# A two-layer hybrid backbone on one core: the z projection between state-space steps, activation tables loaded at the norms, output groups ahead of the last mixer transposes, and head norms of the delta rule in three parts

## The chip, the cores and the metric

The kernel runs on one core of one Trainium2 chip. The metric is the device time of one execution in microseconds (us). The profile names the engines PE (TensorE, matmuls), PEld (its weight loads), DVE (VectorE), ACT (ScalarE), POOL (GpSimd) and SP (SyncE, which issues the weight transfers).

## What is computed

Two trunk layers over 256 context tokens and 256 latent tokens of width 1024, all in fp32. Layer 0 mixes tokens with Mamba-2 (SSD) heads and gated linear attention (GLA) heads side by side, layer 1 with the gated delta rule (GDN). Each layer has a modulated RMS norm ahead of the mixer and of the SwiGLU part, and one RMS norm ends the whole. Scans run forward and backward. The parts that matter here:

```python
def ssd_scan(xdt, da, bm, cm, s0):      # chunked Mamba-2
    ac = jnp.cumsum(da.reshape(b, nc, CHUNK, g, e), axis=2)
    decay = jnp.exp(jnp.where(tril[:, :, None, None], seg, -jnp.inf))
    scores = jnp.einsum('bclgn,bcsgn->bclsg', cc, bc)[..., None] * decay
    y_diag = jnp.einsum('bclsge,bcsgep->bclgep', scores, xc)
    states = jnp.einsum('bclgn,bclgep->bcgepn', bc, xc * to_end[..., None])
...
def even_mixer(...):
    z, xbc, dt_f, dt_b, q, k, v, r, gl_f, gl_b = split_cols(h @ w_in, EV_SPLITS)
...
    y = (y_ssd + d_skip[:, None] * xs).reshape(b, t, SSD_INNER) * jax.nn.silu(z)
    y = rms_norm(y.reshape(b, t, SSD_GROUPS, SSD_INNER // SSD_GROUPS), ...)
    o = rms_norm(y_gla, gla_nw).reshape(b, t, GLA_VAL) * jax.nn.silu(r)
    return jnp.concatenate([y, o], axis=-1) @ w_out
...
def reference(...):
    for i in range(DEPTH):              # 0: even mixer, 1: odd mixer (gated delta rule)
        hl = rms_norm(x, norm_mix[i]) * (1.0 + sc1) + sh1
        x = x + g1 * yl
        x = x + g2 * swiglu(rms_norm(x, norm_ffn[i]) * (1.0 + sc2) + sh2, ffn_w1[i], ffn_w3[i], ffn_w2[i])
    return rms_norm(x, final_norm)
```

## The kernel before

Each engine has its own hand-written program; semaphores join them. Activations are kept transposed, features on the partitions and the 512 tokens along the row, in 8 chunks of 128 features. Weights come in blocks of up to 1 MB through a ring of three slots (RING = 3): SP issues block n as soon as block n-3 is released (lines 647 to 664). A block is released when its two outputs are done ("done"), when it is the first half of something ("used"), or when modulation rows are done ("rows"). A group of a projection (gemm, line 719; gemm_tok, line 753) is one block: two PSUM outputs, f = 0 and f = 1, of 8 chunks each. An fp32 matmul shows as two records of PE. Outputs go round the PSUM banks 0 to 3; a bank is free again when ScalarE or VectorE has drained it.

The stages of layer 0 in TensorE's order: four modulation blocks with the first norm's sums, xbc (6 groups with convolution and transposes), small0, z0 (4 groups), the SSD loop (line 912), qk0 (4 groups), the transposes of the SSD output, v0 (4 groups, each behind a gates() product), r0 (4 groups, each behind the transposes of one key head), the GLA loop, its transposes, out0, the feed-forward stages ff0 and dn0. Layer 1: small1, qkv, z1, the GDN loop, transposes, out1, ff1, dn1. The remaining eight modulation pieces of layer 0 come as 16 late halves (line 690): each is a weight block of its own and 8 short records, put behind f = 0 of a group (between, line 711); LATE_AT gives the places. Before every second one, late_columns(q) turns a row into columns.

The SSD loop has 32 steps u: 8 tiles (4 per direction) of 2 groups of 2 half groups. A step is: POOL makes g_decay (line 2231), TensorE a decay product (line 923), ScalarE Exp (line 1411), VectorE the masked product p_seg (line 1908), TensorE four diagonal products (line 941). Every second step adds a pair: the product with the state (for k > 0) and the new state (lines 945 to 950). VectorE folds a pair into y0 and st0 (accumulate, line 1879). At every fourth step it makes the inputs xdt and xw (line 1872), of which there is one buffer each, after the accumulation of the step before. TensorE's order at a step is decay(u+1), wait for p_seg(u), diagonal products, pair.

Behind the loop VectorE multiplies y0 by z, ScalarE sums squares and makes the norm's scale (lines 1412 to 1417), VectorE scales y0 in 8 products (merged). Then VectorE takes the gates gk of v0 (line 1925), one for each gates() product of TensorE, which waits for the one before (line 966).

A norm (ScalarE, line 1326) waits for the residual of each chunk, squares it, TensorE sums (norm_sum), then ScalarE does Ln and Exp; VectorE scales and ScalarE shifts the chunks of hT one by one, and the first group behind the norm waits for each chunk in its f = 0 part (line 733). The tables of ScalarE are loaded by ACT_TABLE_LOAD, which the compiler puts ahead of an activation whose function is not in the loaded set.

In the GDN loop ScalarE squares the outputs of chunk 6 in steps 28 to 31 (line 1695), and after the loop makes the scales of its 16 heads, squares chunk 7, and makes the scales of those (lines 1697 to 1700). VectorE merges, TensorE transposes 16 tiles, and ScalarE copies each (mixed, line 1419). out0 and out1 have 16 chunks in two blocks per group; the first block reads tiles 0 to 7, which for out0 are SSD tiles.

## Time and profile before

| | us |
|---|---|
| median of 3 runs | 2292.64 (2291.91 to 2293.5) |
| the profiled execution | 2295.65 |
| its span in the trace | 2293.8 |
| PE busy | 2089.5 |
| DVE busy | 729.5 |
| ACT busy | 566.1 |

A row of the timeline has its start, its duration, the engine, the line, the operation, output<-input, the shape and type, the count of merged records, and in brackets how long the engine had been idle and what ended that. A row of the windows has the stretch, its length, the busy time of PE, PEld, DVE, ACT and POOL with the number of records, the granted TensorE clock as a share of full speed (0.50 is 1.2 GHz, 1.00 is 2.4 GHz), the busy share of the DMA engines and GB/s. Row times are us from the start of the span.

### The profile page before, as it was taken

The page shows a single profiled execution, that of the slowest core. Times are in us where ns is not written, and L with a number is a line of the kernel's source. Part 1 is how long each engine was busy: PE and PEld are TensorE (multiplying, and loading weights), DVE is VectorE, ACT ScalarE, POOL GpSimd, SP SyncE. Part 2 cuts the span into 40 slices and gives each one's busy share as a digit, 9 for nine tenths or more (in the row PEclk, how much of TensorE's full clock was granted, in tenths as well). Part 3 has the DMA queues.
Part 4 walks back from the last instruction along what each step waited for, and adds up shares of the span by engine and source line. Part 5 has one row for each costly group of instructions (what it writes and reads, how often), then busy time and mean ns, then how long its engine had stood idle before and what let it go on. Part 6 is the DMA issues. An engine that isn't in the chain of part 4 may idle for free.

```text
span 2293.8 us, 29492 instructions
## 1 busy us (share of the span) xinstructions
PE 2089.5 (91%) x12486; PEld 1289.4 (56%) x12486; DVE 729.5 (32%) x1474; ACT 566.1 (25%) x1217; POOL 79.6 (3%) x86
## 2 busy tenths in 40 slices
PE   6999766999999799999999998999898889799997
PEld 2468443488555544444444446544576556578886
DVE  2540665000444500100000004555686944210001
ACT  4121112141334400200000004222536766420001
POOL 0000220000000000000000000000102110000000
PEclk9999887999989899999999997999998999799999
DMA  6333000312343122122221122221120001134442
GB/s 250 147 115 147 1 0 2 148 55 108 122 158 148 38 74 83 55 73 73 78 87 69 64 70 77 92 74 55 56 75 3 2 2 56 55 119 157 147 146 93
DMA packets 28000, 193.53 MB, mean 84 GB/s; under 512 B 3004, under 2 KB 4285, under 8 KB 5854
## 3 DMA queue, kind: packets, MB, share of 16 engines
q1 hardware_dynamic: 27826, 191.51, 22.7%
q8 instruction: 99, 1.62, 0.3%
q14 instruction: 31, 0.25, 0.0%
q10 hardware_dynamic: 44, 0.14, 0.0%
HBM read 190.59 MB, written 1.05 MB: 84 GB/s over the span
## 4 chain that ended last, share of the span: by engine, by line
PE 81%; DVE 11%; ACT 5%; issue 2%; DMA 1%; POOL 0%; SPq 0%; ACTq 0%; DVEq 0%; POOLq 0%
PE psum L673 80%; DVE ws_sb L1746 4%; ACT ws_sb L1312 2%; DVE gl_tmp_sb L1746 1%; DVE arena_sb L1746 1%; DVE hT_sb L1749 1%; ACT L1312 1%; ACT arena_sb L1312 1%; ACT wide_sb L1312 1%; DVE ws_sb L1749 1%; DMA xT_sb<-x 1%; DVE ring_sb L1746 1%; ACT const_sb L1312 1%; ACT hT_sb L1312 0%; DVE arena_sb L1755 0%
## 5 line engine op out<-in xcount | busy, mean ns | idle before, releaser
L673 PE MATMUL psum<-hT_sb,ring_sb 128*128 128x512 f32 (+1 forms) x2256 | 810.6, 522 | 19.4 <-ACT hT_sb L1312 15.0
L673 PEld LDWEIGHTS psum<-hT_sb,ring_sb 128*128 128x128 f32 x2256 | 433.7, 193 | 389.3 <-issue 357.0
L673 PE MATMUL psum<-arena_sb,ring_sb 128*128 128x512 f32 (+1 forms) x1216 | 396.3, 488 | 3.6 <-DVE small_sb L1752 1.9
L1312 ACT ACTIVATE ws_sb<-psum 128x512 f32<-128x512 f32 (+3 forms) x268 | 148.6, 554 | 860.8 <-PE psum L673 853.1
L673 PEld LDWEIGHTS psum<-arena_sb,ring_sb 128*128 128x128 f32 x1216 | 232.7, 192 | 165.3 <-issue 144.1
L673 PE MATMUL psum<-ring_sb,hT_sb 128*128 128x256 f32 (+4 forms) x1312 | 251.8, 378 | 11.3 <-ACT hT_sb L1312 11.3
L673 PEld LDWEIGHTS psum<-ring_sb,hT_sb 128*128 128x128 f32 (+1 forms) x1312 | 207.8, 187 | 56.9 <-issue 20.0
L673 PE MATMUL psum<-ws_sb 128*32 128x32 f32 (+5 forms) x2352 | 143.4, 234 | 46.8 <-DVE ws_sb L1746 46.4
L673 PEld LDWEIGHTS psum<-ws_sb 128*32 128x32 f32 (+4 forms) x2352 | 117.3, 134 | 86.3 <-DVE ws_sb L1746 60.3
L1746 DVE TENSOR_TENSOR arena_sb<-ws_sb,psum 128x512 f32<-128x512 f32 (+1 forms) x44 | 24.4, 555 | 419.9 <-PE psum L673 419.9
L1749 DVE SCALAR_TENSOR_TENSOR xT_sb<-psum,mod_sb,xT_sb 128x256 f32<-128x256 f32 x48 | 23.2, 484 | 388.3 <-PE psum L673 387.7
L1312 ACT ACTIVATE wide_sb<-xT_sb 128x512 f32<-128x512 f32 (+1 forms) x40 | 21.8, 544 | 429.7 <-PE psum L673 296.2
L1749 DVE SCALAR_TENSOR_TENSOR ws_sb<-ws_sb,cols_sb 128x512 f32<-128x512 f32 (+1 forms) x176 | 123.8, 703 | 6.3
L673 PE MATMUL psum<-const_sb,arena_sb 64*128 64x256 f32 (+3 forms) x512 | 104.7, 418 | 6.2 <-ACT const_sb L1312 2.4
L673 PE MATMUL psum<-arena_sb,ws_sb 64*64 64x128 f32 (+1 forms) x640 | 97.6, 316 | 2.9 <-DVE ws_sb L1749 2.7
L673 PE MATMUL psum<-wide_sb,const_sb 128*32 128x256 f32 (+2 forms) x384 | 77.0, 476 | 20.4 <-DVE ws_sb L1755 5.8
L1312 ACT ACTIVATE arena_sb<-psum 128x512 f32<-128x512 f32 x56 | 33.4, 597 | 228.3 <-PE psum L673 221.4
L673 PEld LDWEIGHTS psum<-const_sb,arena_sb 64*128 64x128 f32 (+2 forms) x512 | 55.6, 188 | 49.2 <-issue 37.8
L673 PE MATMUL psum<-ws_sb,const_sb 128*64 128x256 f32 (+1 forms) x192 | 62.0, 540 | 18.7 <-ACT hT_sb L1312 15.4
L1312 ACT ACT_TABLE_LOAD x50 | 64.2, 1283 | 52.6 <-PE psum L673 33.3
L673 PEld LDWEIGHTS psum<-arena_sb,ws_sb 64*64 64x64 f32 (+1 forms) x640 | 64.4, 154 | 13.1 <-issue 7.2
L2216 POOL TENSOR_TENSOR wide_sb<-small_sb,const_sb 128x512 f32<-128x512 f32 x24 | 25.5, 1060 | 1331.8 <-PE psum L673 1317.6
(154 smaller groups left out, 1404.7 us busy)
## 6 DMA issues: line engine op xcount, KB each, us to landing
ring_sb<-w SPq DMA_DIRECT2D x170, 1024.0 KB, 4.8
ring_sb<-w SPq DMA_DIRECT2D x8, 768.0 KB, 4.0
xT_sb<-x SPq DMA_DIRECT2D x1, 2048.0 KB, 14.0
...
ring_sb<-w SPq DMA_DIRECT2D x2, 256.0 KB, 4.1
...
```

Of the source, the lines that this page charges most:

```text
L673: return nc.tensor.matmul(o, l, r, start=start, stop=stop)
L1312: return nc.scalar.activation(o, i, func, **kw)
L1746: return V.tensor_tensor(o, a, b, op)
L1749: return V.scalar_tensor_tensor(out=o, in0=a, scalar=sc, in1=b, op0=op0, op1=op1)
L2216: return G_.tensor_tensor(o, a, b, ALU.mult)
```

## The change

- z0 leaves its place ahead of the SSD loop. It is cut into 32 parts of 4 matmuls; parts 0 and 1 come ahead of the loop, part u+2 at step u between decay(u+1) and the wait for p_seg(u). ScalarE copies each of the 8 fills (z_copy) and applies Silu to all of z behind the loop. qk0 takes the place ahead of the loop.
- xdt and xw have two buffers; inputs(m+1) are made at step 4m+1. Each accumulation comes behind the next masked product. The state and the state product have one PSUM bank each instead of two, since z uses banks 2 and 3.
- The transposes of the SSD output and their copies move behind v0.
- The 16 late halves are placed anew: xbc 8 (two each in groups 4 and 5), qk0 4, r0 4.
- load_tables(5) at the start of every norm, behind z's Silu, behind the last GLA squares, and ahead of the last GDN squares.
- gemm_after: the first group behind mix0, ffn0 and ffn1 does both outputs for each chunk; small1 and the first query group are done together, chunk by chunk. Norms wait for drained banks in place of the "residual" count. The Sigmoid of beta comes behind Ln.
- out0's first block is multiplied ahead of the GLA transposes, out1's first block behind 10 of the 16 GDN transposes.
- The GDN squares begin at step 25; the scales of chunk 6 are made at step 29, those of 12 heads of chunk 7 behind the loop, the last four after that, and the merges of chunk 6 go into steps 30 and 31.

```diff
+LN_TABLES = 5
...
-LATE_AT = {"xbc": (0, 6), "z0": (6, 4), "qk0": (10, 4), "r0": (14, 2)}
+LATE_AT = {("xbc", 0): (0,), ("xbc", 1): (1,), ("xbc", 2): (2,), ("xbc", 3): (3,), ("xbc", 4): (4, 5), ("xbc", 5): (6, 7),
+           ("qk0", 0): (8,), ("qk0", 1): (9,), ("qk0", 2): (10,), ("qk0", 3): (11,),
+           ("r0", 0): (12,), ("r0", 1): (13,), ("r0", 2): (14,), ("r0", 3): (15,)}
...
+        if outs_end == "z":
+            self.n_z += 2
+            release = ("z", self.n_z)
...
-    with_late("z0", 4)
     with_late("qk0", 4)
+    p.stage("z0", [([(CB, KC)], "z")] * 4)
...
-        z0 = area(arena, 4096, TT, D)
+        z0 = area(arena, 0, TT, D)
...
-        xdt = area(ws, 5120, SSD_H, SSD_P)
-        xw = area(ws, 6144, SSD_H, SSD_P)
+        xdt = [area(w, at, SSD_H, SSD_P) for w, at in ((ws, 5120), (extra, 0))]
+        xw = [area(w, at, SSD_H, SSD_P) for w, at in ((ws, 6144), (extra, 1024))]
...
-        gate = ws[0:2 * RANK + 1, 1024:2048]
+        gate = extra[0:2 * RANK + 1, 2048:3072]
...
-                if n == plan.stages["z0"][0][0][0]:
+                if n == plan.stages["qk0"][0][0][0]:
                     sp.dma_start(const[:, 6:NCONST - 1, :], consts[:, 6:NCONST - 1, :]).then_inc(s_levels, 16)
...
-                if n % 2 == 0 and n > 0:
+                if n % 2 == 0 and n not in (0, 12):
                     late_columns(n // 2 - 1)
...
+                for half in LATE_AT.get((stage, g), ()):
+                    late_half(half)
+
+            def gemm_after(stage, src, lo, tag):
+
+                ids, first = plan.stages[stage][0]
+                w = slot(ids[0], CB, KC)
+                block_ready(ids[0])
+                for f in range(2):
+                    bank_free(first + f)
+                for c in range(KC):
+                    chunk_ready(tag, c)
+                    for f in range(2):
+                        last = mm(psum[:, (first + f) % 4, lo:T], w[:, c, f * P:(f + 1) * P], src(c),
+                                  start=(c == 0), stop=(c == KC - 1))
+                        if c == KC - 1:
+                            last.then_inc(s_done, 1)
+                between(stage, 0)
...
+                        if meanwhile:
+                            meanwhile()
...
+                    src = lambda c, s=span(stage, 2 * g): hT[:, c, s]
+                    if g > 0:
+                        gemm(stage, g, src, KC, lo=span(stage, 2 * g).start)
+                    elif stage == "xbc":
+                        gemm_after(stage, src, 0, "mix0")
...
-            def small1():
+            def small1_and_first_queries():
+
                 ids, b = plan.stages["small1"][0]
                 w = slot(ids[0], 64, KC)
                 block_ready(ids[0])
                 bank_free(b)
-                for j in range(TT):
-                    for c in range(KC):
-                        if j == 0:
-                            chunk_ready("mix1", c)
-                        last = paired_mm(psum[:, b % 4, j * 64:(j + 1) * 64], c, j, w[:, c, :])
-                last.then_inc(s_done, 1)
+                q_ids, first = plan.stages["qkv"][0]
+                wq = slot(q_ids[0], CB, KC)
+                block_ready(q_ids[0])
+                for f in range(2):
+                    bank_free(first + f)
+                s = span("qkv", 0)
+                for c in range(KC):
+                    chunk_ready("mix1", c)
+                    for j in range(TT):
+                        last = paired_mm(psum[:, 4 + j, 0:64], c, j, w[:, c, :])
+                    if c == KC - 1:
+                        last.then_inc(s_done, 1)
+                    for f in range(2):
+                        last = mm(psum[:, (first + f) % 4, s], wq[:, c, f * P:(f + 1) * P], hT[:, c, s],
+                                  start=(c == 0), stop=(c == KC - 1))
+                        if c == KC - 1:
+                            last.then_inc(s_done, 1)
...
+            def z0_part(n):
+
+                fill, sub = n // 4, n % 4
+                g, f, bank = fill // 2, fill % 2, 2 + fill % 2
+                block = plan.stages["z0"][g][0][0]
+                w = slot(block, CB, KC)
+                if sub == 0:
+                    if f == 0:
+                        block_ready(block)
+                    if fill >= 2:
+                        pe.wait_ge(S["z_taken"], fill - 1)
+                j = 2 * f + sub // 2
+                for c in range(sub % 2 * 4, sub % 2 * 4 + 4):
+                    last = mm(psum[:, bank, sub // 2 * CB:(sub // 2 + 1) * CB], hT[:, c, j * P:(j + 1) * P], w[:, c, :],
+                              start=(c == 0), stop=(c == KC - 1))
+                if sub == 3:
+                    last.then_inc(S["z_done"], 1)
...
-                pe.wait_ge(S["late_copied"], 5)
-                pe.wait_ge(S["late_taken"], 4)
+                late_columns(5)
                 edges(0)
+                pe.wait_ge(S["late_taken"], 6)
...
                 last.then_inc(S["ssd_bc"], 1)
+                for g in (2, 3):
+                    for i in range(2):
+                        drained(pe, out_of("qk0", g, i))
+                z0_part(0)
+                z0_part(1)
                 pe.wait_ge(S["ssd_masked"], 4)
                 pe.wait_ge(S["edge"], 1)
...
+                    if u + 2 < 32:
+                        z0_part(u + 2)
...
+                        if v > 0:
+                            pe.wait_ge(S["ssd_y"], v)
                         if k > 0:
-                            mm(psum[:, 2 + v % 2, :], cT[:, g, j * P:(j + 1) * P], st0[:, g])
-                        last = mm(psum[:, v % 2, :], b_tok[:, j, g * P:(g + 1) * P],
-                                  xw[:, g * 8:(g + 1) * 8].rearrange("p a b -> p (a b)"))
+                            mm(psum[:, 1, :], cT[:, g, j * P:(j + 1) * P], st0[:, g])
+                        last = mm(psum[:, 0, :], b_tok[:, j, g * P:(g + 1) * P],
+                                  xw[m % 2][:, g * 8:(g + 1) * 8].rearrange("p a b -> p (a b)"))
...
-                for j in range(2 * D_FF // CB):
-                    gemm(f"ff{i}", j, lambda c: hT[:, c, lo:T], KC, lo=lo, after=f"ffn{i}" if j == 0 else None)
+                gemm_after(f"ff{i}", lambda c: hT[:, c, lo:T], lo, f"ffn{i}")
+                for j in range(1, 2 * D_FF // CB):
+                    gemm(f"ff{i}", j, lambda c: hT[:, c, lo:T], KC, lo=lo)
...
             for g in range(4):
-                gemm_tok("z0", g, (0, 1, 2, 3))
+                gemm("qk0", g, lambda c: hT[:, c, :], KC)
             ssd()
...
-            pe.wait_ge(S["late_taken"], 6)
+            pe.wait_ge(S["ssd_exp"], 32)
+            pe.wait_ge(S["z_taken"], 8)
             for g in range(4):
                 gates(g)
+                if g == 1:
+                    pe.wait_ge(S["ssd_y"], 16)
                 gemm_tok("v0", g, (0, 1, 2, 3))
+            transpose_mix("ssd", y0, 8, TT)
             pe.wait_ge(S["gk"], TT)
+            pe.wait_ge(S["mixed"], 8)
             for g in range(4):
                 key_tokens(g)
                 gemm_tok("r0", g, (0, 1, 2, 3))
+            late_columns(LATE - 1)
             gla()
-            transpose_mix("gla", o0, 8, TT)
-            pe.wait_ge(S["mixed"], 16)
-            gemm_and_norm("out0", lambda c: mixT[:, c, :], 16, "ffn0")
...
+
+            def gla_transposes():
+                transpose_mix("gla", o0, 8, TT)
+                pe.wait_ge(S["mixed"], 16)
+
+            pe.wait_ge(S["gla_taken"], 16)
+            gemm_and_norm("out0", lambda c: mixT[:, c, :], 16, "ffn0", gla_transposes)
             ffn(0)
-            small1()
+            small1_and_first_queries()
...
-            transpose_mix("gdn", o1, 16, 2)
-            pe.wait_ge(S["mixed"], 32)
-            gemm_and_norm("out1", lambda c: mixT1[:, c, :], 16, "ffn1")
+
+            def gdn_transposes():
+                transpose_mix("gdn", o1, 16, 2, 10)
+                pe.wait_ge(S["mixed"], 32)
+
+            transpose_mix("gdn", o1, 10, 2)
+            pe.wait_ge(S["mixed"], 24)
+            gemm_and_norm("out1", lambda c: mixT1[:, c, :], 16, "ffn1", gdn_transposes)
...
+            def load_tables(n):
+
+                nc.scalar.add_instruction(mybir.InstLoadActFuncSet(name=nc.get_next_instruction_name(), ins=[], outs=[], act_func_set_id=n))
...
+                load_tables(LN_TABLES)
...
-                        act.wait_ge(S["residual"], (n - 1) * KC + c + 1)
+                        drained(act, out_of(NORM_OF[tag], c // 2, c % 2))
...
+            def z_copy(fill):
+
+                act.wait_ge(S["z_done"], fill + 1)
+                g, f_ = fill // 2, fill % 2
+                own(f(z0[:, 2 * f_:2 * f_ + 2, g * CB:(g + 1) * CB], psum[:, 2 + fill % 2, :].rearrange("p (a b) -> p a b", a=2),
+                      ACT.Copy).then_inc(S["z_taken"], 1), S["z_taken"])
...
+                    if u % 4 == 3:
+                        z_copy(u // 4)
+                for i in range(2):
+                    z = z0[:, 2 * i:2 * i + 2]
+                    ins = f(z, z, ACT.Silu)
+                own(ins.then_inc(S["z_ready"], 1), S["z_ready"])
+                load_tables(LN_TABLES)
...
-            def gla():
...
+                    if stage == "r0":
+                        mixed("ssd", 8, 0, lambda t: cl("ssd_norm", t), mixT, T)
...
+                load_tables(LN_TABLES)
...
-                link(f(beta, beta, ACT.Sigmoid))
                 log1p_exp_neg_abs(te, das, S["ab_ln"])
+                own(f(beta, beta, ACT.Sigmoid).then_inc(S["beta"], 1), S["beta"])
...
+                    if i >= 25:
+                        squares(6 + (i - 25) // 4, (i - 25) % 4)
+                    if i == 29:
+                        head_scales(16, 32)
+                head_scales(0, 12)
+                load_tables(LN_TABLES)
+                squares(7, 3)
+                head_scales(12, 16)
...
+            act.dma_start(gate, gate_in).then_inc(s_gate, 16)
+            keys_and_queries()
...
+                def inputs(m):
+
+                    d, k = m // 4, m % 4
                     j = TILE_AT[d][k]
                     xj = x0[:, j].rearrange("p (h c) -> p h c", c=SSD_P)
-                    link(tt(xdt, xj, bc(dt[:, j, d * 16:d * 16 + 16], 2, SSD_P), ALU.mult))
-                    own(tt(xw, xdt, bc(edge[:, j, d * 16:d * 16 + 16], 2, SSD_P), ALU.mult).then_inc(S["ssd_x"], 1), S["ssd_x"])
+                    link(tt(xdt[m % 2], xj, bc(dt[:, j, d * 16:d * 16 + 16], 2, SSD_P), ALU.mult))
+                    own(tt(xw[m % 2], xdt[m % 2], bc(edge[:, j, d * 16:d * 16 + 16], 2, SSD_P), ALU.mult).then_inc(S["ssd_x"], 1), S["ssd_x"])
...
+                inputs(0)
                 for u in range(32):
                     d, k, g, hq = u // 16, u // 4 % 4, u // 2 % 2, u % 2
-                    if u % 4 == 0:
-                        if u > 0:
-                            accumulate(u // 2 - 1)
-                        inputs(d, k)
                     dve.wait_ge(S["ssd_exp"], u + 1)
                     if u - 1 > 0:
                         dve.wait_ge(S["ssd_diag"], u - 1)
                     own(tt(p_seg[:, u % 2], e_seg[:, u % 2], bc(g_mask[:, d, g, TILE_AT[d][k]], 1, 4), ALU.mult).then_inc(S["ssd_p"], 1), S["ssd_p"])
-                    if u % 4 == 3:
+                    if u % 2 == 0 and u > 0:
                         accumulate(u // 2 - 1)
+                    if u % 4 == 1 and u < 28:
+                        inputs(u // 4 + 1)
                 accumulate(15)
+                dve.wait_ge(S["z_ready"], 1)
...
+                def merge(i, heads):
+
+                    dve.wait_ge(S["mix_rs"], 3 if i == 1 else 4 if heads[0] < 12 else 5)
+                    for h in heads:
+                        o = o1[:, i, h * P:(h + 1) * P]
+                        ins = stt(o, o, stat[:, i * 16 + h:i * 16 + h + 1], z1[:, i, h * P:(h + 1) * P], ALU.mult, ALU.mult)
+                        if i == 0:
+                            own(ins.then_inc(S["merged"], 1), S["merged"])
...
+                    if i >= 30:
+                        merge(1, range(8 * (i - 30), 8 * (i - 29)))
+                merge(0, range(12))
+                merge(0, range(12, 16))
...
+            dve.wait_ge(S["beta"], 1)
```

## Rows read from the trace of the kernel before

**Rows 1.** Page, parts 1 and 4: busy time and chain.

```profile
PE 2089.5 (91%) x12486; PEld 1289.4 (56%) x12486; DVE 729.5 (32%) x1474; ACT 566.1 (25%) x1217; POOL 79.6 (3%) x86
...
PE 81%; DVE 11%; ACT 5%; issue 2%; DMA 1%; POOL 0%; SPq 0%; ACTq 0%; DVEq 0%; POOLq 0%
```

**Rows 2.** Windows by stage: stretch, its us, busy us by engine, PEclk, DMA.

```profile
158.10:219.50 61.40, 61.40 (x304) 50.91 (x304) 8.18 (x20) 10.94 (x17) 2.08 (x2) 1.00 0.31 120
...
227.60:386.40 158.80, 104.80 (x377) 64.31 (x376) 99.86 (x120) 19.11 (x32) 32.19 (x30) 0.81 0.00 1
386.40:450.30 63.90, 63.87 (x176) 27.59 (x177) 10.30 (x11) 14.23 (x29) 0.00 (x0) 0.96 0.26 101
...
457.50:523.40 65.90, 65.84 (x277) 53.02 (x278) 4.90 (x4) 26.01 (x28) 0.00 (x0) 0.97 0.14 48
...
781.90:798.80 16.90, 6.34 (x33) 4.79 (x33) 9.73 (x22) 9.60 (x16) 0.00 (x0) 0.70 0.01 1
...
1953.00:1978.70 25.70, 9.29 (x32) 4.68 (x33) 10.61 (x33) 20.73 (x60) 0.00 (x0) 0.54 0.00 0
```

**Rows 3.** Timeline, TensorE: late modulation half, z group, one SSD period.

```profile
181.01 1.04 PE L673 MATMUL psum<-ring_sb,small_sb 128*2 128x512 f32 x8
181.98 14.08 PE L673 MATMUL psum<-ring_sb,hT_sb 128*128 128x256 f32 x64
...
271.42 1.97 PE L673 MATMUL psum<-ws_sb 128*128 128x64 f32 x8 [7.20 <-DVE ws_sb L1746]
...
276.14 1.94 PE L673 MATMUL psum<-ws_sb,arena_sb 128*128 128x512 f32 x4
```

**Rows 4.** Timeline, VectorE, the same SSD period.

```profile
268.16 1.22 DVE L1746 TENSOR_TENSOR ws_sb<-arena_sb,small_sb 128x1024 f32<-128x1024 f32 x1
...
275.98 0.96 DVE L1746 TENSOR_TENSOR ws_sb<-ws_sb 128x512 f32<-128x512 f32 x1 [3.88 <-ACT ws_sb L1312]
...
280.70 0.69 DVE L1746 TENSOR_TENSOR ws_sb<-psum,small_sb 128x512 f32<-128x512 f32 x1
...
288.40 1.23 DVE L1746 TENSOR_TENSOR ws_sb<-arena_sb,small_sb 128x1024 f32<-128x1024 f32 x1
```

**Rows 5.** Timeline behind the SSD loop: VectorE and ScalarE.

```profile
386.41 4.42 DVE L1746 TENSOR_TENSOR arena_sb<-arena_sb 128x4096 f32<-128x4096 f32 x1
...
396.95 1.28 ACT L1312 ACT_TABLE_LOAD   x1
...
400.17 5.78 DVE L1746 TENSOR_TENSOR arena_sb<-arena_sb,small_sb 128x512 f32<-128x512 f32 x8 [9.33 <-ACT small_sb L1312]
...
464.21 1.23 DVE L1749 SCALAR_TENSOR_TENSOR arena_sb<-psum,ws_sb 128x1024 f32<-128x1024 f32 x1 [36.41 <-ACT ws_sb L1312]
```

**Rows 6.** Two large transfers at 107.7 to landing; page part 6, small ones.

```profile
DMA to landing us min/median/max: 4.7/5.8/6.9
...
ring_sb<-w SPq DMA_DIRECT2D x2, 256.0 KB, 4.1
```

**Rows 7.** Table load behind ffn0's sum (timeline); windows of the first feed-forward group.

```profile
916.08 1.28 ACT L1312 ACT_TABLE_LOAD   x1 [1.26 <-PE psum L673]
...
921.80:927.50 5.70, 5.62 (x7) 2.50 (x8) 5.31 (x12) 5.37 (x11) 0.00 (x0) 0.50 0.00 0
927.50:938.70 11.20, 11.20 (x27) 4.95 (x26) 0.86 (x2) 3.58 (x6) 0.00 (x0) 1.00 0.00 0
```

**Rows 8.** Windows: small1, then the first queries of layer 1.

```profile
1401.20:1410.50 9.30, 9.30 (x68) 8.95 (x69) 0.00 (x0) 0.00 (x0) 0.00 (x0) 0.50 0.00 0
1410.50:1428.30 17.80, 17.80 (x78) 15.31 (x77) 10.49 (x31) 8.93 (x16) 0.00 (x0) 0.85 0.34 122
```

**Rows 9.** Timeline at the two mixer ends.

```profile
788.22 8.30 DVE L1749 SCALAR_TENSOR_TENSOR hT_sb<-hT_sb,small_sb,arena_sb 128x256 f32<-128x256 f32 x16 [4.15 <-ACT small_sb L1312]
...
1953.59 1.28 ACT L1312 ACT_TABLE_LOAD   x1
...
1966.84 6.16 DVE L1749 SCALAR_TENSOR_TENSOR hT_sb<-hT_sb,small_sb,arena_sb 128x128 f32<-128x128 f32 x16 [5.73 <-ACT small_sb L1312]
```

123 lines of the change are left out of this document (42 added, 81 removed).

## The prediction

> **What bounds the kernel now.** I read the page's busy shares and its chain first. TensorE is busy 91% of the span and carries 81% of the chain; VectorE carries 11%, ScalarE 5% [rows 1]. So two things can pay: stretches in which TensorE stands idle or runs slowly, and work that can be moved into them. The stages come next [rows 2]. The state-space (SSD) loop, 227.6 to 386.4, is the one large hole: 158.8 us, of which TensorE is busy 104.8, at a granted clock of 0.81. The z projection just before it (158.1 to 219.5) and the key and query projection behind it (386.4 to 450.3) are solid matmuls. The other holes are the two mixer ends, 16.9 us with 6.3 busy and 25.7 with 9.3 busy.
>
> **Inside the SSD loop.** Between two tiles TensorE waits 7.20 us for VectorE [rows 3]. VectorE then runs in a row the two accumulations of a tile, the two input products and the next masked product: the input product starts at 268.16 and again at 288.40, a period of 20.24 us for four steps [rows 4]. The work of VectorE in a period is 4 masked products of 0.96, 2 accumulations of 5 operations (0.69 to 0.99, together 3.75 with their gaps) and 2 products of 1.23: 13.9 us. TensorE's is, at full clock, 4 decays of 0.86 (two records of 0.43; the pair of four takes 1.77 from start to start), 4 diagonal groups of 0.86 to 1.0 and 2 pairs of 1.77: 10.5. The loop is bound by neither, but by their taking turns.
>
> **1. z into the loop, queries before it.** The whole z projection is 128 matmuls; 32 of them (64 records) take 14.08 us, one part of four 1.72 [rows 3], 32 parts 55. New loop on TensorE at full clock: 55 + 32 decays 27.5 + 32 diagonals 27.5 + 16 pairs 24.8 (four have half the work) = 134.8. Is it then bound by TensorE? Let a pair end at 0. TensorE does decay, part and diagonal until 3.4, decay and part until 6.0, then needs the masked product. VectorE starts its accumulation at 0.1, ends at 3.85, and has the product at 4.85: 1.2 us to spare. The next pair needs that accumulation (one bank instead of two), there since 3.85. With the double xdt and xw the inputs (2.5) follow, the next product is ready at 8.35, and the pair ends at 8.65. So yes. Added: 2.5 for the first parts at the half clock at which the stage before ends, 2.1 at the end, where steps 30 and 31 have no part to fill them. 139.4 from the end of the B-C products (227.6) to the last pair. ScalarE's eight z copies (0.6) and two Silu have room: it is busy 19.1 of 158.8 [rows 2].
> What hid the rest before was the query stage, and it is gone from there. Behind the last pair VectorE accumulates (3.8), multiplies by z (4.42); ScalarE sums squares (6.0, until the load at 396.95), then Ln, an Exp load and Exp 1.8 (its Ln load now lies ahead: 1.28 less); VectorE merges 5.8 [rows 5] and only then, in order, takes the first gate tile, 1.23: done at 23.4. ScalarE's gate work (4.5) ends at 20.7, inside that. TensorE has two gate matmuls, 1.9, and the first value group, 14.0: at 15.9 it reaches the second gates, which wait for that tile. A new stall of 7.5, and 2.3 of half clock after it. Value stage: 4 x 15.9 + 9.8 = 73.4, against 65.8 [rows 2]; the 8 SSD transposes cost 7.1 as before.
> Sum from 227.6 to the start of r0: before 523.4 - 227.6 = 295.8, after 139.4 + 73.4 + 7.1 = 219.9: **-75.9**. The query stage ahead of the loop takes the z stage's place with the same 128 half-length matmul times and four late halves: 0.
>
> **2. The late halves of the modulation.** Sixteen as before; two more with a column step go to xbc, a column step to the SSD head, two halves to r0: +5.6 (0.97 a half [rows 3], 0.87 a column step), which the -75.9 had counted as removed. But xbc groups 4 and 5 now carry two halves each, and the ring has three slots. The block of group 5 is then the third behind that of group 4 and can only be asked for when group 4 is done; before, one other block lay between. The transfer lands 4.7 us after its issue [rows 6], 0.2 is issue, 0.87 of transposes hide it: 4.0 us of wait. The same for the small block behind group 5: the page's two such transfers have a median of 4.1 [rows 6], one of them behind a large one (5.7), so 2.5 alone: 1.8 of wait. Half clock after them: 2.7. **+8.5** (+4 to +12). On SP's queue the level masks (2 MB) are now issued behind the small block; the next weight block behind them has the small projection's 17 us. The last column step ends r0: +0.5.
>
> **3. Tables early at the norms.** Each norm has a load of 1.28 for Ln between the sum of squares and Ln (916.08), and another for Exp [rows 7]. The first now runs while ScalarE waits for the squares: five norms x 1.28 = **-6.4**. In the gated-attention scales the load still follows the last squares in ScalarE's order: 0. The removed "residual" step was not last in its wait: 0.
> The record of a load is 1.28 and the Ln starts at once after it. The Trainium skill, ScalarE: Activation LUTs, "What ACT_TABLE_LOAD costs", adds a drain of 1.38 to every switch; by it the five would give 13.3 and the sum would be some 7 us lower. The rows show no such gap.
>
> **4. Both halves of the first group per chunk.** The old first half was paced by the norm's chunks, 1.07 us each, so 8.7 instead of 7.0. But TensorE comes out of the norm's idle time at the half clock: 5.7 us at 0.50 behind ffn0 [rows 7]. Old: one group until 938.7, 16.9 us. New: 16 x 0.87 + half of 5.7 = 16.8. The wait for chunks had hidden the half clock; now it shows. **0** at mix0, ffn0 and ffn1 (-1.5 to +0.5 each).
>
> **5. small1 with the first queries.** The small projection runs 9.3 us at clock 0.50 with TensorE full, and the first query groups still have part of the half clock (0.85 over 17.8 us) [rows 8]. New, a chunk is 12 small records (0.10 hot, 0.14 cold) and 4 of 0.215: 1.9 hot, 3.4 cold. From 1391.3, a chunk and a half cold and the others hot: first group done at 1409.4, 10.7 before the old 1420.1. The second group, the edge sums, then the third group at 1417.7, which needs the first bank drained: ScalarE's chain behind small1 sheds two loads (no switch to the sigmoid and back), and that is at 1416.6. Old 1428.3: **-10.6**, 1.3 of it the Ln load counted in 3: **-9.3** here. Of this -2 to -10 is open, since what clock the mix gets no row shows.
>
> **6. Output groups ahead of the transposes.** At out0 TensorE idles from 781.9, while ScalarE and VectorE make the norm and merge (788.22, 8.30 us) [rows 9]. The first half of group 0 reads only SSD tiles: 16 x 0.87 = 13.9, from 783.6 to 797.5; then the 8 transposes 7.2, to 804.7, where the old kernel has that half done at 812.7: **-8.0**.
> At out1 ScalarE's chain is the limit: after the loop (1953.59) a pair of loads with the first norm, 16 squares, a second pair, and merges from 1966.84 [rows 9]. New: the first two parts go into the loop, where ScalarE has 1.6 to 2.1 us free per step and squares need 1.75; the scales at step 29 (3.1) do not fit and push the end by 2. Then scales of 12 heads until 1958.6, a load, 4 squares, the last scales until 1963.5, and only then the copies of the transposes, which are behind them in ScalarE's order. Ten tiles until 1970.2, first half 7.0 + 1.8, six tiles 4.1: 1983.3 against 1987.5: **-4.2** (-6 to 0).
>
> **Sum.** The terms: -75.9 + 5.6 + 8.5 + 0.5 - 6.4 - 9.3 - 8.0 - 4.2 = -89.2. The profiled execution took 2295.65 us (span 2293.8, the rest lies around it): 2206.4. The median of the runs is 3.0 below that execution: 2203.4, say 2203.5.
>
> **Rivals.** (a) The loop keeps its turns: some wait I did not see takes the place of the removed one, and four steps still take 20.2 (for: one bank now serves every pair; against: 1.2 us spare): loop 162, +22: 2226. Chance 0.10. (b) **Slower than before**: the parts do not lift the clock. At half clock a part is 3.4, a decay 1.7, a diagonal 1.8, a pair 3.5: 17.3 a pair, 277 for the loop: 2341. It decides from a loop of 229 us on, 7.1 a step. Against: the z stage of the same matmuls ran at 1.00 [rows 2]. 0.03. (c) The early load does nothing, because the Ln load is placed again: +6.4 and 1.3 behind the loop: 2211. 0.07. (d) The mix of 5 stays at the half clock: 8 x 3.4 = 27 instead of 18: 2212. 0.10. (e) One load serves Ln and Exp, and the Exp loads go too, about eight on the path, 9 us: 2194. That is the rule of the Trainium skill, ScalarE: Activation LUTs, "Table sets: the hidden batching unit": a set exists that holds both. The trace has two loads wherever Exp follows Ln [rows 7], and the diff names one set only. 0.05. The forecast as worked out has 0.65.
>
> **Chances.** Faster by over 0.2% (about what a measurement here can tell from no change) 0.96, same 0.01, slower 0.03. Range: ring waits, clock and mixer ends move the sum by -10 to +12, and (a), (c), (d), (e) lie at 2194 to 2226: 2190 to 2226.
>
> **What would show it.** TensorE near full at clock 1.0 in the loop, about 139 us to the last pair; a wait of 7 to 8 us before the second gates; waits for ring_sb of 4 and 2 us around xbc group 5; one table load, not two, behind each norm's sum; no gain in the first group of ffn0. It is wrong if the loop's TensorE still waits for masked products, or if the clock stays at 0.5 in loop or mix.

## The result: 2228.8 us, 63.5 faster, where 89 were forecast

| | before | changed | ratio, 95% |
|---|---|---|---|
| median | 2292.27 (4 runs) | 2228.82 (4 runs, 2223.81 to 2232.25) | 0.9722 (0.970 to 0.9745) |
| the same kernels, measured again | 2293.21 | 2226.86 (4 runs, 2219.6 to 2229.96) | 0.9697 (0.9672 to 0.9722) |
| profiled execution, its span | 2295.65, 2293.8 | 2232.25, 2230.4 | |

The forecast was 2203.5, with a range of 2190 to 2226; the time lies 2.8 us above its upper end. Below, experiments are compared with the changed kernel by their ratios to the kernel before; its own is taken as 0.971, the middle of the two, and 0.001 is 2.3 us. With intervals of about 0.002 each, a difference of 6 us or less between two of them is not told apart by times, and is read from the traces.

Page of the changed kernel, parts 1 and 4, as [rows 1] of before:

```profile
PE 2088.2 (94%) x12486; PEld 1288.1 (58%) x12486; DVE 724.1 (32%) x1442; ACT 571.8 (26%) x1221; POOL 88.1 (4%) x86
...
PE 85%; DVE 7%; ACT 5%; issue 1%; DMA 1%; POOL 0%; SPq 0%; ACTq 0%; DVEq 0%; POOLq 0%
```

TensorE's busy time is what it was (2089.5), in a span 63 us shorter: idle time went, and VectorE's share of the chain fell (11% to 7%). The DMA engines have 1% of the chain in both pages; in the changed kernel a part of it is the weight ring (`DMA ring_sb<-w 1%` by line), which the page of before does not list among its lines of 1%.

Where the time went, by the start of the same instruction in each trace. The changed kernel has two traces:

| stretch | forecast | first trace | second trace |
|---|---|---|---|
| start to xbc | -1.3 | -1.6 | -1.1 |
| xbc, to the small projection | +8.6 | +12.2 | +11.8 |
| small projection to the B-C products (their half clock was booked with the ring) | +3.6 | +6.5 | +5.7 |
| B-C products to GLA | -73.5 | -70.8 | -71.8 |
| GLA loop | 0 | +6.2 | +1.7 |
| out0 up to Exp of ffn0 | -9.3 | -9.6 | -9.6 |
| to Exp of mix1 | -1.3 | -1.2 | -1.1 |
| small1 and qkv | -9.3 | +4.3 | +4.3 |
| GDN, out1, to Exp of ffn1 | -5.5 | -6.8 | -6.7 |
| to the end | -1.3 | -2.7 | -2.7 |
| sum | -89.3 | -63.5 | -69.5 |

One edit that was to give 9.3 costs 4.3: 13.6 of the 26 us missed. The rest is in the stages ahead of the loop (6.5), in GLA (6.2 or 1.7) and between the B-C products and GLA (2.7 or 1.7), against some 3 us gained beyond the forecast at the other norms and mixer ends.

**The state-space loop** did what was forecast. Windows of the changed kernel (columns as in [rows 2]) and its timeline of one pair:

```profile
244.90:385.20 140.30, 137.53 (x634) 100.60 (x633) 96.94 (x115) 30.20 (x44) 40.58 (x30) 0.99 0.09 31
```

```profile
254.15 1.89 PE L680 MATMUL psum<-ring_sb,hT_sb 128*128 128x256 f32 x8
255.88 1.00 PE L680 MATMUL psum<-ws_sb 128*128 128x64 f32 x8
256.72 1.08 PE L680 MATMUL psum<-ws_sb,arena_sb 128*128 128x512 f32 x2
257.63 1.02 PE L680 MATMUL psum<-ws_sb,const_sb 128*128 128x512 f32 x2
258.49 1.89 PE L680 MATMUL psum<-ring_sb,hT_sb 128*128 128x256 f32 x8
260.21 1.00 PE L680 MATMUL psum<-ws_sb 128*128 128x64 f32 x8
```

Part (1.73 from start to start), diagonal, new state, decay, part: no idle time in brackets, where [rows 3] has 7.20. 140.3 us at clock 0.99 against 139.4 forecast.

**The waits of TensorE** between xbc and GLA, longest first (what was waited for, us in total, times, longest), and the value stage:

```profile
PE psum L680 <- DVE arena_sb L1838: 6.8, 1, 6.8
PE psum L680 <- DMA ring_sb<-w: 6.2, 2, 4.0
PE psum L680 <- ACT hT_sb L1384: 3.0, 1, 3.0
PE psum L680 <- DVE ws_sb L1835: 2.8, 1, 2.8
```

```profile
401.29 5.77 DVE L1835 TENSOR_TENSOR arena_sb<-arena_sb,small_sb 128x512 f32<-128x512 f32 x8 [7.99 <-ACT small_sb L1384]
407.09 1.22 DVE L1838 SCALAR_TENSOR_TENSOR arena_sb<-psum,ws_sb 128x1024 f32<-128x1024 f32 x1
408.37 3.78 PE L680 MATMUL psum<-extra_sb,gl_tmp_sb 33*128 33x512 f32 x4 [6.80 <-DVE arena_sb L1838]
412.08 16.41 PE L680 MATMUL psum<-ring_sb,hT_sb 128*128 128x256 f32 x64
```

The 6.8 is the predicted wait before the second gates (7.5): VectorE merges 5.77, then takes the gate tile, then TensorE goes on. Behind it a value group takes 16.41 instead of 14.08 and the gate product 3.78 instead of 1.98: 4.1 of half clock, where I had 2.3. The ring's waits were forecast as 4.0 and 1.8 and are 4.04 and 2.14.

**The mix** of small1 and the first queries, timeline and window:

```profile
1334.45 1.74 PE L680 MATMUL psum<-ring_sb,hT_sb 128*64 128x64 f32 x12 [4.78 <-ACT hT_sb L1384]
1335.98 2.02 PE L680 MATMUL psum<-hT_sb,ring_sb 128*128 128x256 f32 x4
1337.93 2.14 PE L680 MATMUL psum<-ring_sb,hT_sb 128*64 128x64 f32 x12
```

```profile
1334.40:1365.40 31.00, 30.95 (x130) 22.00 (x131) 9.14 (x22) 7.25 (x15) 0.00 (x0) 0.51 0.03 6
```

TensorE is busy 30.95 of 31.0 us, and yet its clock stays at the lower of its two levels: 3.88 a chunk, eight times. All nine traces of kernels with this mix behind this norm have it at the low clock, with lengths within 0.7 us of each other. This was rival (d), at 4 us worse than its price of 27.

### The profile page after: what moved, and what is told of

It reads as the page before. It is cut to its first block, busy times and chain, and to the rows that moved or that the text cites. A ratio compares the mean times of both kernels' runs of the same rounds, so it can differ in the third digit from the quotient of the medians.

```text
span 2230.4 us, 29470 instructions
## 1 busy us (share of the span) xinstructions
PE 2088.2 (94%) x12486; PEld 1288.1 (58%) x12486; DVE 724.1 (32%) x1442; ACT 571.8 (26%) x1221; POOL 88.1 (4%) x86
## 4 chain that ended last, share of the span: by engine, by line
PE 85%; DVE 7%; ACT 5%; issue 1%; DMA 1%; POOL 0%; SPq 0%; ACTq 0%; DVEq 0%; POOLq 0%
PE psum L680 85%; ACT ws_sb L1384 2%; DVE ws_sb L1835 1%; DVE gl_tmp_sb L1835 1%; DVE arena_sb L1835 1%; ACT arena_sb L1384 1%; DMA ring_sb<-w 1%; DMA xT_sb<-x 1%; DVE ws_sb L1838 1%; ACT L1384 1%; ACT wide_sb L1384 1%; ACT const_sb L1384 1%; DVE ring_sb L1835 0%; ACT hT_sb L1384 0%; DVE arena_sb L1844 0%
## 5 line engine op out<-in xcount | busy, mean ns | idle before, releaser
L680 PE MATMUL psum<-ring_sb,hT_sb 128*128 128x256 f32 (+4 forms) x1312 | 263.4, 382 | 6.9 <-ACT hT_sb L1384 4.8
L680 PEld LDWEIGHTS psum<-ring_sb,hT_sb 128*128 128x128 f32 (+1 forms) x1312 | 212.3, 189 | 70.5 <-issue 34.5
L680 PE MATMUL psum<-ws_sb 128*32 128x32 f32 (+5 forms) x2224 | 115.2, 225 | 0.2 <-issue 0.2
L680 PE MATMUL psum<-arena_sb,ws_sb 64*64 64x128 f32 (+1 forms) x640 | 104.0, 329 | 3.0 <-DVE ws_sb L1838 2.7
L680 PEld LDWEIGHTS psum<-ws_sb 128*32 128x32 f32 (+4 forms) x2224 | 90.2, 124 | 14.8 <-issue 9.0
L680 PEld LDWEIGHTS psum<-arena_sb,ws_sb 64*64 64x64 f32 (+1 forms) x640 | 68.2, 160 | 15.4 <-issue 7.5
L680 PE MATMUL psum<-ws_sb,const_sb 128*64 128x256 f32 (+1 forms) x192 | 51.6, 474 | 15.5 <-ACT hT_sb L1384 15.5
## 6 DMA issues: line engine op xcount, KB each, us to landing
xT_sb<-x SPq DMA_DIRECT2D x1, 2048.0 KB, 13.9
```

What stands on the lines that cost most here:

```text
L680: return nc.tensor.matmul(o, l, r, start=start, stop=stop)
```

## The experiments

In short: the forecast's terms for the state-space loop, the waits of the ring, the gates and the mixer ends hold; the mix fails by its cold start alone; and the waits that the change leaves are removable, down to 2177 us.

### Which parts give what: e1, e2, e3, e12

e1_z_alone keeps the z parts and the late halves and takes everything else back. e2_small1_alone takes back the mix, e3 the explicit loads, e12 the ends of both mixers (for GDN the old squares from step 28 and two `head_scales`, too). e1 is these three together with the old first groups:

```diff
-            small1_and_first_queries()
+            small1()
...
             def load_tables(n):
-                nc.scalar.add_instruction(...)
+                pass
...
-            pe.wait_ge(S["gla_taken"], 16)
-            gemm_and_norm("out0", lambda c: mixT[:, c, :], 16, "ffn0", gla_transposes)
+            gla_transposes()
+            gemm_and_norm("out0", lambda c: mixT[:, c, :], 16, "ffn0")
...
-            transpose_mix("gdn", o1, 10, 2)
-            pe.wait_ge(S["mixed"], 24)
+            transpose_mix("gdn", o1, 16, 2)
+            pe.wait_ge(S["mixed"], 32)
```

> Parts 1 and 2 alone: the z projection in the state-space loop and the new places of the late halves; everything else (early tables, both halves of a first group per chunk, small1 with the first queries, output groups ahead of transposes, head norms in three parts) is as in the kernel before. By the terms of the forecast: 2292.3 - 75.9 + 5.6 + 8.5 + 0.5 = 2231. By the trace of the changed kernel: between the starts of xbc and r0 it is 54.0 us shorter, r0 is 1.9 longer, and the GLA loop behind it, the same instructions, 6.2 longer. If those 6.2 belong to the change: 2292.3 - 54.0 + 1.9 + 6.2 = 2246; if they are only where the clock happened to fall in that execution: 2240.

Measured 2238.57, ratio 0.9757 (0.9735 to 0.9779), 56 us faster than before; the trace's GLA loop took 194.3. So the z move gives some 56 of the 61 forecast for it, and the 6.2 of GLA do not follow from z alone.

> The changed kernel with the small projection of layer 1 by itself again and the first query group behind it. By the forecast's step 5 this is 9.3 us slower than the changed kernel: 2238. By the trace of the changed kernel, where the mix ran at a clock of 0.50 from its first record to its last and a chunk took 3.88 us, the edit of step 5 cost 3.4 us instead of giving 9.3: this kernel should be 3.4 us faster, 2225.

Measured 2221.04, ratio 0.9671 (0.9648 to 0.9694): 9 us faster than the changed kernel, not slower. From the Exp of mix1 to the first GDN mask it takes 255.9 us; the changed kernel 260.4, the kernel before 256.1. 4.5 of the 9 are the mix; the others lie in stages that the edit does not touch.

> The changed kernel without its explicit table loads; where ScalarE needs a table it is loaded at the use. By the forecast's step 3: five norms at 1.28 and one load behind the state-space loop, 6.4 to 7.7 slower, 2235 to 2236.5. By a drain of 1.38 added to every switch, as the Trainium skill (ScalarE: Activation LUTs, What ACT_TABLE_LOAD costs) has it, 13 to 16 slower, 2242 to 2245. If the scales of GDN gain from their explicit load too, 1.3 more.

Measured 2233.92, ratio 0.9728 (0.9705 to 0.975), 4 us slower. In the traces each norm is 1.3 slower: TensorE waits 4.21, 5.88 and 4.91 us for the first chunk behind mix0, ffn0 and ffn1, against 2.96, 4.60 and 3.64. The last stretch is 2.3 longer, of which 1.1 is the clock in the feed-forward products behind ffn1 (154.7 against 153.6). Nothing like 13 to 16: the drain of 1.38 that the Trainium skill has (ScalarE: Activation LUTs, "What ACT_TABLE_LOAD costs") is not seen here.

> The changed kernel with both mixer ends as before: all transposes ahead of out0 and out1, and the head norms of the delta rule in two parts. By the forecast's step 6: 8.0 + 4.2 = 12.2 slower than the changed kernel, 2241. By the traces: out0 up to the norm behind it 8.3 to 9.6, out1 and the loop ahead of it 4.4 to 5.1: 13 to 15 slower, 2242 to 2244. If the three parts of the head norms cost in the loop what they give behind it, 8: 2237.

Measured 2234.57, ratio 0.9735 (0.9709 to 0.9761), 6 us slower, no more than the scatter. By the traces: from the GLA loop to the Exp of ffn0 137.3 against 129.3, 8.0, as forecast. From the first GDN mask to the Exp of ffn1 it took 391.1; eleven traces with the new end and table set 5 took 385.1 to 390.3, 387.6 on average: 3.5, where 4.2 was forecast. That difference is smaller than the scatter of the stretch, and the trace of the changed kernel (390.2) happens to be at its upper end.

### What filling the loop gives: e10

```diff
-                z0_part(0)
-                z0_part(1)
+                for n in range(32):
+                    z0_part(n)
...
-                    if u + 2 < 32:
-                        z0_part(u + 2)
```

> The changed kernel with all 32 z parts ahead of the state-space loop (55 us) and none in it; the double buffers, the one bank for the pair and the order of VectorE stay as changed. It tells what of the gain is the filling and what the new order. By the forecast's working the new order alone removes the turns: VectorE's 13.9 per four steps then bound the loop, 8 x 13.9 = 111, with z 166, against 140 in the changed kernel: 26 slower, 2255. If the turns stay without the filling (20.2 per four steps, 162, with z 217) it is 77 slower: 2306. Since TensorE idles in the loop, its clock falls in either case; at a clock near 0.8 TensorE's 10.5 become 13, still under VectorE's.

Measured 2259.28, ratio 0.985 (0.9826 to 0.9875): 32 us slower than the changed kernel. Windows of z and of the loop:

```profile
240.00:294.00 54.00, 54.00 (x252) 47.54 (x251) 4.69 (x6) 4.18 (x7) 0.00 (x0) 1.00 0.17 59
294.00:418.00 124.00, 95.76 (x379) 54.86 (x377) 91.25 (x109) 25.65 (x37) 36.13 (x30) 0.91 0.03 9
```

The loop takes 15.5 a period of four steps: neither the 20.2 of the turns nor VectorE's 13.9. The new order and the double buffers gave 4.7 a period, 38 us; filling gave the rest, 178 - 140 = 38, of which 32 are left in the time of the whole. What holds a period at 15.5 is not shown here.

### The ring: e4

One late half in each xbc group, half 6 behind the last group, half 7 between the two parts of the small projection:

```diff
-LATE_AT = {("xbc", 0): (0,), ("xbc", 1): (1,), ("xbc", 2): (2,), ("xbc", 3): (3,), ("xbc", 4): (4, 5), ("xbc", 5): (6, 7),
+LATE_AT = {("xbc", 0): (0,), ("xbc", 1): (1,), ("xbc", 2): (2,), ("xbc", 3): (3,), ("xbc", 4): (4,), ("xbc", 5): (5,),
...
+                        if (stage, g) == ("xbc", 5):
+                            late_half(6)
...
                 last.then_inc(s_done, 1)
+                late_half(7)
                 bank_free(b + 1)
```

> The changed kernel with one late half in each xbc group, one behind the last xbc group and one between the two parts of the small projection, so that no two of these blocks stand between two large ones. The trace of the changed kernel has waits of 4.04 and 2.14 us for the ring and 1.8 us of half clock behind the first. If the ring of three is their cause they go, but for about 1 us ahead of the small projection: 7 us faster, 2222. If the transfers were limited by the memory rather than by the release of a slot, the same bytes are due in the same time and the waits only move: 2229. If the half clock in the small projection comes from the wait ahead of it, about 3 us more go: 2219; if it comes from its own narrow matmuls, it stays.

Measured 2217.99, ratio 0.9662 (0.964 to 0.9683), 11 us faster than the changed kernel. Its timeline and windows:

```profile
140.02 1.04 PE L684 MATMUL psum<-ring_sb,small_sb 128*2 128x512 f32 x8
140.99 1.09 PE L889 MATMUL psum<-const_sb,arena_sb 128*128 128x128 f32 x8
142.09 10.98 PE L684 MATMUL psum<-ring_sb,hT_sb 128*128 128x32 f32 x64
```

```profile
142.00:144.00 2.00, 1.99 (x18) 1.91 (x18) 1.89 (x4) 0.00 (x0) 0.00 (x0) 1.00 1.00 414
146.00:154.00 8.00, 8.00 (x42) 7.21 (x42) 1.48 (x5) 0.63 (x1) 0.00 (x0) 0.50 0.71 297
```

No wait for the ring is left; the small projection starts 9.3 us sooner (142.09 against 151.37), 1.0 of it because half 7 now comes behind its first part. The release of the slots was the cause, not the memory. But the clock still falls some 3 us into the narrow matmuls, with no idle time ahead, and stays low for some 9 us, against 12.7 in the changed kernel: most of this loss was not the ring's, and my half clock of 2.7 stood under the wrong cause.

### The value stage: e5

```diff
                 own(tt(y0, y0, z0, ALU.mult).then_inc(S["summed"], 1), S["summed"])
+                gate_rows(0)
                 dve.wait_ge(S["mix_rs"], 1)
```

and, on ScalarE, the first `log1p_exp_neg_abs` ahead of the wait for `summed` (the squares then write elsewhere, and the explicit table load at that place goes).

> The changed kernel, but ScalarE does the first gate tile before it waits for the product y0 times z, and VectorE takes that tile between this product and the merges. In the changed kernel TensorE waits 6.8 us for that tile and then runs at half clock, which costs 1.8 in the gate matmuls and 2.3 in the second value group. If the in-order queues of ScalarE and VectorE are the cause, as the forecast had it, all of it goes: 10.9 faster, 2218. If the clock would have fallen there anyway, 6.8 faster, 2222. If the merges, now later, hold up the transposes behind the value stage, less; they are due some 50 us later, so I expect none of that.

Measured 2214.71, ratio 0.964 (0.9627 to 0.9654), 16 us faster. From the first to the last gate product 47.8 against 59.3 us: 11.5, the wait and its half clock, as expected; the other 4 to 5 are elsewhere and within the scatter. VectorE now takes the tile early:

```profile
384.79 4.42 DVE L1835 TENSOR_TENSOR arena_sb<-arena_sb 128x4096 f32<-128x4096 f32 x1
389.25 1.22 DVE L1838 SCALAR_TENSOR_TENSOR arena_sb<-psum,ws_sb 128x1024 f32<-128x1024 f32 x1
396.91 1.98 PE L680 MATMUL psum<-extra_sb,gl_tmp_sb 33*128 33x512 f32 x4
397.27 5.78 DVE L1835 TENSOR_TENSOR arena_sb<-arena_sb,small_sb 128x512 f32<-128x512 f32 x8 [6.80 <-ACT small_sb L1384]
```

### One table for Ln and Exp: e7

```diff
-LN_TABLES = 5
+LN_TABLES = 6
```

> The changed kernel with table set 6 in place of set 5 in its explicit loads. The Trainium skill (ScalarE: Activation LUTs, Table sets: the hidden batching unit) says that one set holds both Ln and Exp. By my rival (e) the Exp loads behind the explicit ones go: five norms, the SSD scales, the GLA scales and the last GDN scales, 8 loads of 1.28, of which 7 to 8 are on the path: 9 to 10 faster, 2219. By the other reading the compiler puts its own load ahead of Exp whatever set is in: no change, 2229.

Measured 2217.54, ratio 0.9652 (0.9635 to 0.9668), 13 us faster. ScalarE at ffn0, first the changed kernel, then e7:

```profile
860.39 0.69 ACT L1384 ACTIVATE wide_sb<-psum,eps_col_sb 128x512 f32<-128x512 f32 x1 [1.27 <-PE psum L680]
861.09 1.28 ACT L1384 ACT_TABLE_LOAD   x1
862.39 0.63 ACT L1384 ACTIVATE wide_sb<-wide_sb 128x512 f32<-128x512 f32 x1
```

```profile
856.94 0.69 ACT L1384 ACTIVATE wide_sb<-psum,eps_col_sb 128x512 f32<-128x512 f32 x1 [1.27 <-PE psum L680]
857.66 0.63 ACT L1384 ACTIVATE wide_sb<-wide_sb 128x512 f32<-128x512 f32 x1
```

Rival (e) is not what the changed kernel does, whose trace still has a load between Ln and Exp; with set 6 the second load goes, 16 loads in all (35 against 51). The Trainium skill (ScalarE: Activation LUTs, "Table sets: the hidden batching unit") says that one set holds both Ln and Exp, so that Ln and then Exp need one load; the trace agrees.

### Why the mix stayed at half clock: e6b, e13, e16

e6b: the first query group alone behind the norm, then the small projection by itself, then the second group. e13: the first group alone, then the mix, with the second group. e16: the changed kernel's mix, with five matmuls nobody reads in the wait ahead of it. The edits of e6b and of e16 (e13 has the mix, with the second group, in place of `small1()`):

```diff
+                    else:
+                        gemm_after(stage, src, 0, "mix1", span(stage, 0))
+                        small1()
```

```diff
+                if tag in WARM:
+                    lo = NORMS[tag][2] * CTX
+                    for c in range(WARM[tag]):
+                        mm(psum[:, 7, lo:T], ones, xT[:, c % KC, lo:T])
```

> The changed kernel with the first query group alone behind the norm, both outputs for each chunk, then the small projection by itself, then the second query group; ScalarE copies the first tile ahead of the small projection's chain. Two readings of the mix, which stayed at clock 0.50: (1) the idle time of the norm holds the clock down and any matmuls lift it after some 6 us: then the first query group ends hot, some 12 us behind the norm, the 96 records of the small projection take 0.10 each, 9.6, and the second group 8.2: edge sums 30 us behind the start, against 38 in the changed kernel and 34.4 in the order of before, 8 faster than the changed kernel: 2221. (2) The narrow matmuls themselves bring the clock down: the small projection starts hot and falls to 0.50, 0.14 a record for most of it: edge sums at 33, 5 faster: 2224.

> The first query group alone behind the norm, as in e6b, and then the mix of step 5, chunk by chunk, with the second query group instead of the first: the same instructions that ran at clock 0.50, 3.88 us a chunk, now begun at clock 1.00. If the mix as such brings the clock down, it falls within a few us and the mix takes near 8 x 3.88 = 31 us, 18 longer than the 13.2 that e6b needed for the two parts one after the other: 2227. If only the start counts, and a mix begun at 1.00 stays there, the mix takes the 6.1 + 7.1 = 13.2 to 15 of the parts: within 2 us of e6b, 2209 to 2211.

> The changed kernel with five extra matmuls of 512 columns (0.87 each at full clock) into an unused bank while TensorE would wait 4.8 us for the norm ahead of the mix of step 5; their result is not used. If it is only the cold start that held the mix at 0.50, it now starts and stays at 1.00: it is then paced by the chunks, 1.24 each, and then by its own 2.18 a chunk as in e13: 8 x 2.18 = 17.5 instead of 31: 13 faster, 2214. If the short rest of the gap (0.4 us) is enough to bring the clock down, or the mix falls on its own, no change: 2227.

Measured: e6b 2209.21, ratio 0.9615 (0.9599 to 0.9631), 22 us faster than the changed kernel. e13 2222.25, 0.9697 (0.968 to 0.9713), 3 faster. e16 2212.05, 0.9642 (0.9619 to 0.9665), 16 faster. From Exp of mix1 to the first mask: 245.0, 256.5 and 245.9, against 260.4. TensorE in e6b, in e13 and in e16 (timeline and window):

```profile
1328.75 9.78 PE L684 MATMUL psum<-hT_sb,ring_sb 128*128 128x256 f32 x32 [4.77 <-ACT hT_sb L1378]
1338.46 6.09 PE L684 MATMUL psum<-ring_sb,hT_sb 128*64 128x64 f32 x96
```

```profile
1342.62 1.08 PE L684 MATMUL psum<-hT_sb,ring_sb 128*128 128x256 f32 x4
1343.63 1.33 PE L684 MATMUL psum<-ring_sb,hT_sb 128*64 128x64 f32 x12
```

```profile
1324.93 4.46 PE L681 MATMUL psum<-xT_sb,const_sb 128*128 128x512 f32 x10
1329.89 1.33 PE L681 MATMUL psum<-ring_sb,hT_sb 128*64 128x64 f32 x12 [0.50 <-ACT hT_sb L1389]
1331.06 1.08 PE L681 MATMUL psum<-hT_sb,ring_sb 128*128 128x256 f32 x4
```

```profile
1329.90:1347.30 17.40, 17.40 (x129) 13.00 (x130) 8.23 (x17) 7.00 (x14) 0.00 (x0) 1.00 0.01 2
```

The first query group and what follows it in e6b (windows):

```profile
1328.80:1332.40 3.60, 3.60 (x9) 2.91 (x10) 3.38 (x7) 2.93 (x7) 0.00 (x0) 0.53 0.00 0
1332.40:1344.50 12.10, 11.96 (x121) 9.69 (x120) 5.06 (x8) 4.42 (x9) 0.00 (x0) 1.00 0.26 89
```

The same instructions take 3.88 a chunk begun at the low clock and 2.18 begun at the full one, and stay there: it is the cold start alone, and 4.46 us of unread matmuls in the wait remove it. The query group of 256 columns in e6b came out of the same idle time and was at 1.00 some 4 us later, so it is the mix that did not lift the clock, though it held it. What in the mix keeps it from lifting the clock was not taken apart. e6b gave 15.4 us in its stretch where its better reading had 8: the first query group came out of the low clock sooner, and the 96 records took 6.1 instead of 9.6. e13 shows the second reading, a mix that stays at 1.00, but at 17.5 us and not 13 to 15; the rest of its gain was spent on a wait of 4.6 us ahead of the edge sums, whose inputs the mix makes late, and on the half clock behind it. The Trainium skill (TensorE: Matmul & The Clock Gate, "What's actually happening") says that the clock rises once TensorE has been busy for a while; here a TensorE that was busy all the time stayed low for 31 us, and the measurement decides.

### Narrow work in the small projection: e14

The 16 wide records of its second part are put between the four tiles of the first.

> The changed kernel with the second part of the small projection of layer 0 (16 records of 512 columns) put between the four tiles of its first part (64 records of 32 columns). In the changed kernel and in e4_ring, which has no wait ahead of it, the clock fell from 1.00 to 0.50 some 3 us into the first part and stayed there for about 10. If an unbroken run of narrow matmuls is what brings it down, breaking it keeps the clock up and the stage is 3 to 5 us shorter: 2223. If the clock falls for the share of narrow work in a stretch, mixed or not, the low clock now also covers the wide records, which cost twice as much there: 0 to 4 us longer, 2228 to 2231.

Measured 2224.49, ratio 0.971 (0.9692 to 0.9728): no change. The clock fell there too, for 9.4 us against 12.7:

```profile
153.00:162.40 9.40, 9.40 (x24) 4.31 (x22) 0.78 (x2) 0.61 (x1) 0.00 (x0) 0.53 0.76 319
```

An unbroken narrow run is not needed for the fall. Why this mix falls from the full clock and that of e13 does not stays open.

### Controls: e9, e15

> The changed kernel once more, unaltered, for a second time and a second trace. If the 6.2 us that the GLA loop was longer than before belong to the change, its 201.0 us come again; if they are where the clock falls in an execution, any length between 194 and 201. Time 2224 to 2232 either way.

> The kernel before, unaltered, for a second trace of it. Its GLA loop took 194.8 us in the first; the same loop took 194.3 to 201.0 in the traces since. If the length is a matter of where the clock falls, any of these; if the kernel before leads into it in a way that spares dips, 194 to 196 again.

e9: 2226.86; e15: 2295.79, ratio 1.0005. Their GLA loops, and that of the first trace of the changed kernel:

```profile
530.20:729.60 199.40, 180.92 (x2352) 113.99 (x2352) 101.65 (x248) 82.30 (x201) 0.00 (x0) 0.91 0.36 137
```

```profile
587.80:785.40 197.60, 179.22 (x2352) 112.57 (x2352) 101.61 (x248) 82.31 (x201) 0.00 (x0) 0.92 0.35 134
```

```profile
532.00:735.90 203.90, 185.73 (x2352) 117.20 (x2352) 101.68 (x248) 82.33 (x201) 0.00 (x0) 0.89 0.35 134
```

The same 2352 records: busy 179.2 to 185.7, and only the clock differs. Up to its last products the loop took 194.8 in both traces of before, 201.0 and 196.5 in those of the changed kernel, and 194.3 to 201.0 in the others. The clock falls once in most of the loop's 16 steps (147 records each), and a step that escapes is 1.1 to 1.7 us shorter than the same step with a fall. So 4.5 of the 6.2 vary between executions of one kernel. Whether the remaining 1.7 belong to the change stays open: e1, with z in the loop, had 194.3, and all sixteen other traces of kernels with the change had 196.5 or more.

### All together: e8, e11, e17

e8 joins e4, e5 and e6b; e11 adds e7; e17 adds unread matmuls in three norms.

> The changed kernel with the new places of the late halves (as e4_ring), the first gate tile ahead of the merges (as e5) and the small projection behind the first query group (as e6b). The three sit in stages that do not touch one another, so their gains should add: 10.8 as measured for the first, 10.9 as expected for the second, 5 to 8 for the third: 2199 to 2202. If what each gives is partly a matter of where the clock falls in the later loops, the sum misses by several us either way.

> e8_combined with table set 6 in its explicit loads. The trace of e7_one_table has 35 table loads against 51, each 1.28; on the path are those behind the five norms and at the GLA and GDN scales. From e8_combined's 2185.7 by 9 to 10: 2176. If the path in the combined kernel hides the loads of the state-space end and the gates, which is likely now that TensorE does not wait there, 7: 2179.

> e11_combined_one_table with such extra matmuls in three norms: three of 512 columns ahead of ff0 and of the first query group (2.6 us of a wait of 3.3 to 3.5), five of 256 ahead of ff1. In e11 some 4 us behind each of the first two norms run at 0.50, so 2 us each are to be had: 3 to 5 faster, 2173. The first group behind a norm is paced by chunks anyway, which may hide it: 2177, no change.

| | us | ratio, 95% |
|---|---|---|
| e8 | 2185.72 | 0.9518 (0.95 to 0.9536) |
| e11 | 2177.32 | 0.9485 (0.9466 to 0.9504) |
| e17 | 2179.95 | 0.9504 (0.9481 to 0.9527) |

The three edits of e8 give 44, and singly gave 11, 16 and 22, together 49: they add, within the scatter. That is 13 to 16 us more than was expected of the three, because the second and third gave more than their terms. e11 has the lowest median, 116 us under the kernel before and some 51 under the changed one. e17 brings nothing that the times can tell: TensorE's clock is now 1.00 from the first record behind ffn0, and from the Exp of ffn0 to that of mix1 its trace has 465.2 us against 466.8 in e11, near the 2 expected there; the other two norms gave 0.5 and nothing.

## Why the prediction missed

- **Step 1, z in the loop** (-75.9): right in mechanism and near in size. The loop took 140.3 for 139.4; the wait at the gates 6.8 for 7.5; its half clock 4.1 for 2.3, since the gate matmuls ran at it, too. Rivals (a) and (b) fell.
- **Step 2, late halves and ring** (+14.6): waits as forecast. The term mis-sized is the half clock: the small projection and the edge sums ran 12.7 and 10.2 us at 0.50 (17.0 and 3.4 in the second trace), and the stretch from the one to the B-C products grew by 6.5 (5.7), of which 3.6 were booked. xbc itself grew 3.6 more than booked, 1.8 of it the half clock behind the first wait (8.83 for 7.03 us) and 1.3 the first group. I had read the small projection's 8.97 in before as its price; it held a stretch of half clock (146.0 to 152.6 ran at 0.50), and how long that lasts was not fixed. What sets the length stays open.
- **Step 3, early tables** (-6.4): right; e3 loses 4 +- 6, each norm 1.3. Rival (c) fell, and the drain was not seen.
- **Step 4**: 0, as forecast: the feed-forward products behind ffn0 took 305.3 us against 305.2, those behind ffn1 153.6 against 155.0, and the first xbc group 17.0 and 15.4 in the two traces against 15.7.
- **Step 5, small1 with the first queries** (-9.3): this step failed. "A chunk and a half cold and the others hot" took the clock to rise by itself behind a few us of work. It did not, in 31 us. I had seen the small projection of before run 9.3 us at 0.50 with TensorE full [rows 8], and did not draw from it that such work does not lift the clock. Rival (d) had the case, at a chance of 0.10, which was too small with that row in hand, and at 3.4 a chunk; it is 3.88. The hot price was low as well: 1.9, where its own terms (12 x 0.10 + 4 x 0.215) make 2.06 and the traces have 2.18. The rest of the step was right: with the mix begun at the full clock (e16) the stretch from Exp of mix1 to the first mask took 245.9 against 256.1 before, 10.2 less, where 9.3 was forecast.
- **Step 6**: -8.0 measured as 8.0; -4.2 as some 3.5, inside a scatter of 5, so its size is not shown.
- **The range** lacked two cases at once: it took each rival alone, while the mix, the half clock ahead of the loop and GLA's clock came together. It also had no term for the clock of a loop that the change does not touch, which moved a single execution by 2 to 6 us.
